# Stick-breaking attention of a decoder step: from cumulative matmuls to a scan along the keys

## The reference

```python
def stick_breaking_weights(z, mask):
    log_beta = jax.nn.log_sigmoid(z)
    log_1m = jnp.where(mask, jax.nn.log_sigmoid(-z), 0.0)
    ax = z.ndim - 1
    tail = lax.cumsum(log_1m, axis=ax, reverse=True) - log_1m
    return jnp.where(mask, jnp.exp(log_beta + tail), 0.0)

z = jnp.einsum('bqhd,bkhd->bhqk', q_blk, k) * scale + bias_f
mask = kpos[None, :] < qpos[:, None]
a = stick_breaking_weights(z, mask)
out = jnp.einsum('bhqk,bkhd->bqhd', a, v)
```

## Time and profile before

| | before |
|---|---|
| median of 3 runs | 3159.7 us (3157.42 to 3159.77) |
| the profiled execution | 3158.64 us |
| its span | 3156.9 us |
| busy in the span | PE 2901.3, DVE 1443.7, ACT 756.3, POOL 1062.1 us |
| mean granted TensorE clock | 0.955 |
| attention's share of the span | about 15% |

### The profile page before, as it was taken

How to read it: one execution, slowest core, us unless ns; L and a number is a source line. 1 busy time by engine, 2 the same in 40 slices (tenths; PEclk the granted TensorE clock), 3 DMA queues, 4 the chain that set the end, 5 groups by cost and what they waited for, 6 DMA issues and landing times.

```text
span 3156.9 us, 44614 instructions
## 1 busy us (share of the span) xinstructions
PE 2901.3 (92%) x16032; PEld 2619.6 (83%) x16032; DVE 1443.7 (46%) x2610; ACT 756.3 (24%) x1575; POOL 1062.1 (34%) x932
## 2 busy tenths in 40 slices
PE   5999769999999999899888888888999999999997
PEld 3777449999999999899885555556989999999997
DVE  5699964422332222641438888860033222222226
ACT  4111061200000000231227777750012000000002
POOL 2478923223333223223214444431032232332320
PEclk9999889999999999999999999985699999999999
DMA  3000001111111111144252222212311111111111
GB/s 118 28 28 21 15 27 47 41 47 41 54 44 43 47 41 54 40 142 129 70 159 61 57 70 67 63 60 94 107 47 47 41 47 48 47 45 43 42 53 56
DMA packets 87684, 183.97 MB, mean 58 GB/s; under 512 B 28995, under 2 KB 43715, under 8 KB 87268
## 3 DMA queue, kind: packets, MB, share of 16 engines
q1 hardware_dynamic: 64260, 145.00, 14.4%
q10 hardware_dynamic: 23264, 36.61, 3.8%
HBM read 150.59 MB, written 30.99 MB: 58 GB/s over the span
## 4 chain that ended last, share of the span: by engine, by line
PE 71%; DVE 14%; issue 8%; ACT 5%; POOL 1%; ACTq 1%; DVEq 1%; DMA 0%; POOLq 0%; SPq 0%
PE bank L1228 48%; PE bank L1332 14%; DVE cv L979 3%; DVE s_sb L1136 3%; PE bank L1483 2%; PE bank L1455 2%; PE bank L1273 1%; DVE sh_sb L1148 1%; DVE xg L924 1%; DVE xl L928 1%; PE bank L1434 1%; DVE ssq L914 1%; ACT sh_sb L843 1%; DVE rstd L1127 1%; POOL s_sb L540 1%
## 5 line engine op out<-in xcount | busy, mean ns | idle before, releaser
L1228 PE MATMUL bank<-xh,wh 128*128 128x352 f32 x3456 | 1131.5, 327 | 32.5 <-DVE xl L928 22.9
L1228 PE MATMUL bank<-xl,wh 128*128 128x352 f32 x3456 | 1117.3, 323 | 0.0
L1228 PE MATMUL bank<-xh,wl 128*128 128x352 f32 x3456 | 1117.1, 323 | 0.0
L497 POOL CAST wh<-w_raw 128x1024 fp32r<-128x1024 f32 x188 | 301.5, 1604 | 1635.3 <-PE bank L1228 1374.7
L1228 PEld LDWEIGHTS bank<-xh,wh 128*128 128x128 f32 x3456 | 654.9, 189 | 45.2 <-DVE xl L928 18.4
L1228 PEld LDWEIGHTS bank<-xl,wh 128*128 128x128 f32 x3456 | 657.4, 190 | 1.8 <-issue 1.7
L1228 PEld LDWEIGHTS bank<-xh,wl 128*128 128x128 f32 x3456 | 656.3, 190 | 0.0
L499 POOL TENSOR_TENSOR wl<-w_raw,wh 128x1024 fp32r<-128x1024 f32 x188 | 456.4, 2428 | 15.1
L1046 DVE TENSOR_TENSOR bank<-bank,sg 128x352 f32<-128x352 f32 x132 | 70.3, 533 | 793.3 <-ACT sg L730 793.3
L1332 PE MATMUL bank<-hh,wh 128*128 128x352 f32 x1056 | 344.0, 326 | 16.4 <-DVE x L1057 13.8
L730 ACT ACTIVATE sg<-bank 128x352 f32<-128x352 f32 x132 | 61.4, 465 | 1200.8 <-PE bank L1228 1200.7
(11 more groups left out here) (136 smaller groups left out, 3056.6 us busy)
## 6 DMA issues: line engine op xcount, KB each, us to landing
w_raw<-wstream SPq DMA_DIRECT2D x188, 512.0 KB, 3.4
k_sb<-k_split SPq DMA_DIRECT2D x16, 512.0 KB, 3.4
qh_sb<-q_split SPq DMA_DIRECT2D x64, 128.0 KB, 2.7
ql_sb<-q_split SPq DMA_DIRECT2D x64, 128.0 KB, 2.8
kp<-cache_kt SPq DMA_DIRECT2D x16, 512.0 KB, 3.5
vp<-cache_v SPq DMA_DIRECT2D x16, 512.0 KB, 3.5
x<-x_t ACTq DMA_DIRECT2D x3, 1408.0 KB, 11.9
k_t<-stage ACTq DMA_DIRECT2D x8, 528.0 KB, 2.8
```

The source lines that it names most:

```text
L497: pool.tensor_copy(wh[:, s], w_raw[:, s % RAW]).then_inc(w_hi, 1)
L1228: mm = pe.matmul(out, a[:, slot, w], b[:, k, tgs(tg)], start=(k == 0 and i == 0), stop=(k == KC - 1 and i == 2))
```

## The change

It turns the scores round: 128 queries lie on the partitions and keys run along the free axis. A head's 36 causal blocks of 128 by 128 are packed into nine chunks of 512 columns (`HEAD_CHUNKS`; a tuple is query block, lowest key block, number of blocks), three of which hold two query blocks; a pair is 18 chunks and the whole is 144. For a chunk:

- PE (`att_z`): the scores by two matmuls a segment, and for a segment that holds the diagonal a third of 128 columns that adds -1e30 where the mask is false. Four score banks instead of six.
- ACT (`att_sigmoids`): sigmoid(z) to SBUF and sigmoid(-z) in place in PSUM.
- DVE (`att_rest`): a scan from the last key down, state = state * sigmoid(-z) + 0, with the state of the segment behind as its start; then (`att_weights`) one multiplication of two SBUF tiles, in place.
- PE (`att_turn`): four transposes of 128 by 128 into one of two banks; ACT (`att_evict`) copies them to SBUF; PE (`att_av`) multiplies with the values in four full-precision matmuls of 128 columns. Both heads of a pair add into the same output banks, whose accumulation is begun by one matmul a pair and bank (chunks 0 and 2); the zero columns between the heads' values make that right.
- The output is rounded and subtracted once a pair and bank, in 128 partitions (before: 64 partitions, once a head and half).

POOL makes the mask's source once and has no other attention work. The clip, exponentials and logarithm, the high and low parts, the cumulative matmuls and the carry go. A head's queries now have a buffer for each of the two heads, the biases are loaded once, and SP, ACT and DVE run straight code. The diff, with the removed functions (printed above) and the bookkeeping left out:

```diff
-EXP_CLIP = 2.0 ** 60
+MASKED = -1e30
 DEC_SPLIT = 6
-NZ = 6
-LEAD = 6
+NZ = 4
+LEAD = 5
+AT_TILES = 3
...
+HEAD_CHUNKS = (
+    ((3, 0, 4),), ((0, 0, 1), (2, 0, 3)), ((5, 2, 4),), ((1, 0, 2), (5, 0, 2)), ((4, 1, 4),), ((6, 3, 4),),
+    ((4, 0, 1), (6, 0, 3)), ((7, 4, 4),), ((7, 0, 4),))
+NCHUNK = len(HEAD_CHUNKS)
+NATT = H * NCHUNK
+PAIR = 2 * NCHUNK
+REST_TILE = {3: 0, 5: 1, 1: 2, 4: 0, 6: 1, 7: 2}
+SMALL_REST = {0: 0, 2: P + 1}
+REST_FREE = {0: -2, 1: -7, 2: -2, 3: 0, 4: 1, 5: 4, 7: 4}
+OUT_CHUNK = {NCHUNK + 3: 0, PAIR - 1: 1}
+class Segment:
+    def __init__(self, qb, low, n, off):
+        self.qb, self.low, self.n = qb, low, n
+        self.off = off
+        self.cols = slice(off, off + n * P)
+        self.first, self.last = low + n == qb + 1, low == 0
+def chunk(g):
+    off, out = 0, []
+    for qb, low, n in HEAD_CHUNKS[g % NCHUNK]:
+        out.append(Segment(qb, low, n, off))
+        off += n * P
+    assert off == QT
+    return out
+def place(g):
+    return g // PAIR, g // NCHUNK % 2, g // NCHUNK
...
-        s_sb = sb("s_sb", [P, 3, QT], F32, r)
-        sh_sb = sb("sh_sb", [P, 3, QT], F32R, r)
-        sl_sb = sb("sl_sb", [P, 3, QT], F32R, r)
-        a_sb = sb("a_sb", [P, 3, QT], F32, r)
-        sb("gap", [P, 2 * (T - SEQ)], F32, r)
+        s_sb = sb("s_sb", [P, NZ, QT], F32, r)
+        at_sb = sb("at_sb", [P, AT_TILES, QT], F32, r)
+        q1_sb = [sb("q1h_sb", [P, SEQ], F32R, r), sb("q1l_sb", [P, SEQ], F32R, r)]
+        mask_r = sb("mask_r", [P, P], F32R, r)
...
+    rest_tiles = [ssq[:], xg[:].rearrange("p a t -> p (a t)"), rstd[:]]
+    small_rest = sq[:].rearrange("p a t -> p (a t)")
+    mask_src = small_rest[:, 2 * TG - P:2 * TG]
+    def rest(seg, first, n):
+        if seg.qb in SMALL_REST:
+            tile, base = small_rest, SMALL_REST[seg.qb]
+        else:
+            tile, base = rest_tiles[REST_TILE[seg.qb]], SEQ - (seg.qb + 1) * P
+        return tile[:, base + first:base + first + n]
...
-    Z = banks[0:NZ]
+    Z, TB = banks[0:NZ], banks[NZ:6]
...
+        def load_head(it, e):
+            h, used = 2 * it + e, PAIR * (it - 1) + NCHUNK * (e + 1)
+            wait_count(sp, Att.z, used)
+            sp.dma_start(k_sb[:, e].bitcast(F32), k_scr[h].rearrange("s d t -> (s d) t")).then_inc(Att.k_in[e], 16)
+            for part in range(2):
+                for half in range(2):
+                    sp.dma_start(q_sb[e][part][DH * half:DH * half + DH, :].bitcast(F32), q_scr[h, part])\
+                      .then_inc(Att.q_in[e], 16)
+            wait_count(sp, Att.av, used)
+            sp.dma_start(v_sb[:, :, 2 * DH * e:2 * DH * e + DH],
+                         v_nat[0:SEQ, h * DH:h * DH + DH].rearrange("(b p) d -> p b d", p=P))\
+              .then_inc(Att.v_in[e], 16)
...
+        pool.wait_ge(n_kv.ready, NTG * KC)
+        pool.memset(mask_src, MASKED).then_inc(Att.mask_src, 1)
+        pool.wait_ge(Att.mask_src, 1)
+        pool.affine_select(out=mask_src, in_=mask_src, compare_op=ALU.is_ge, fill=0.0, base=0,
+                           pattern=[[1, P]], channel_multiplier=-1).then_inc(Att.mask_src, 1)
...
+        def att_sigmoids(g):
+            it, e, h = place(g)
+            act.wait_ge(Att.z, g + 1)
+            wait_count(act, Att.turn, g + 1 - NZ)
+            act.activation(s_sb[:, g % NZ], Z[g % NZ][:], ACT.Sigmoid, bias=b_sb[:, h:h + 1]).then_inc(Att.sig, 1)
+            act.activation(Z[g % NZ][:], Z[g % NZ][:], ACT.Sigmoid, bias=nb_sb[:, h:h + 1], scale=-1.0)\
+               .then_inc(Att.keep, 1)
+        def att_evict(g):
+            act.wait_ge(Att.turn, g + 1)
+            wait_count(act, Att.av, g + 1 - AT_TILES)
+            act.activation(at_sb[:, g % AT_TILES], TB[g % 2][:], ACT.Copy).then_inc(Att.at, 1)
+        def att_out(g):
+            it, qt = g // PAIR, OUT_CHUNK[g % PAIR]
+            act.wait_ge(Att.av, g + 1)
+            act.activation(xh[:, it, qt * QT:(qt + 1) * QT], DN[qt][:], ACT.Copy).then_inc(Att.o_hi, 1)
+        act.wait_ge(Att.const, 2)
+        for slot in range(-LEAD, NATT):
+            if 0 <= slot + 1 < NATT:
+                att_evict(slot + 1)
+            if slot + LEAD < NATT:
+                att_sigmoids(slot + LEAD)
+            if slot >= 0 and slot % PAIR in OUT_CHUNK:
+                att_out(slot)
...
+        def att_rest(g):
+            head = place(g)[2]
+            v.wait_ge(Att.keep, g + 1)
+            if g % NCHUNK in REST_FREE:
+                wait_count(v, Att.a, NCHUNK * head + REST_FREE[g % NCHUNK])
+            for seg in chunk(g):
+                if not seg.first:
+                    v.wait_ge(Att.rest, g)
+                initial = 1.0 if seg.first else rest(seg, (seg.low + seg.n) * P, 1)
+                ins = v.tensor_tensor_scan(rest(seg, seg.low * P, seg.n * P)[:, ::-1], Z[g % NZ][:, seg.cols][:, ::-1],
+                                           zero[:].to_broadcast([P, seg.n * P]), initial, ALU.mult, ALU.add)
+            ins.then_inc(Att.rest, 1)
+        def att_weights(g):
+            v.wait_ge(Att.sig, g + 1)
+            v.wait_ge(Att.rest, g + 1)
+            for seg in chunk(g):
+                tile = s_sb[:, g % NZ, seg.cols]
+                ins = v.tensor_tensor(tile, rest(seg, seg.low * P + 1, seg.n * P), tile, ALU.mult)
+            ins.then_inc(Att.a, 1)
+        def att_out(g):
+            it, qt = g // PAIR, OUT_CHUNK[g % PAIR]
+            cols = slice(qt * QT, (qt + 1) * QT)
+            v.wait_ge(Att.o_hi, 2 * it + qt + 1)
+            v.tensor_tensor(xl[:, it, cols], DN[qt][:], xh[:, it, cols].bitcast(F32), ALU.subtract)\
+             .then_inc(Att.o_lo, 1)
         for n in range(2):
             v.wait_ge(q_stored[n], 4 * 16 * (KC // 2))
+        v.wait_ge(Att.mask_src, 2)
+        v.tensor_copy(mask_r[:], mask_src)
+        v.memset(zero[:], 0.0)
+        for tile in rest_tiles:
+            v.memset(tile[:, SEQ:SEQ + 1], 1.0)
+        for qb, base in SMALL_REST.items():
+            v.memset(small_rest[:, base + (qb + 1) * P:base + (qb + 1) * P + 1], 1.0)
+        v.wait_ge(Att.b_in, 16)
+        v.tensor_scalar(nb_sb[:], b_sb[:], -1.0, None, ALU.mult).then_inc(Att.const, 2)
+        v.wait_ge(Att.const, 2)
+        for slot in range(-LEAD, NATT):
+            if 0 <= slot + LEAD - 1 < NATT:
+                att_rest(slot + LEAD - 1)
+            if 0 <= slot + LEAD - 2 < NATT:
+                att_weights(slot + LEAD - 2)
+            if slot >= 0 and slot % PAIR in OUT_CHUNK:
+                att_out(slot)
...
+        def att_z(g):
+            it, e, h = place(g)
+            if g % NCHUNK == 0:
                 pe.wait_ge(Att.k_in[e], it * 16 + 16)
+                pe.wait_ge(Att.q_in[e], it * 64 + 64)
+            wait_count(pe, Att.rest, g + 1 - NZ)
+            for seg in chunk(g):
+                out, keys = Z[g % NZ][:, seg.cols], k_sb[:, e, seg.low * P:(seg.low + seg.n) * P]
+                queries = slice(seg.qb * P, (seg.qb + 1) * P)
+                pe.matmul(out, q_sb[e][0][:, queries], keys, start=True, stop=False)
+                mm = pe.matmul(out, q_sb[e][1][:, queries], keys, start=False, stop=True)
+                if seg.first:
+                    mm = pe.matmul(Z[g % NZ][:, seg.cols.stop - P:seg.cols.stop], ident_r[:], mask_r[:], start=False,
+                                   stop=True, skip_group_check=True)
+            mm.then_inc(Att.z, 1)
+        def att_turn(g):
             pe.wait_ge(Att.a, g + 1)
+            wait_count(pe, Att.at, g - 1)
+            for b in range(QT // P):
+                cols = slice(b * P, (b + 1) * P)
+                mm = pe.transpose(TB[g % 2][:, cols], s_sb[:, g % NZ, cols], ident[:])
+            mm.then_inc(Att.turn, 1)
+        def att_av(g):
+            it, e, h = place(g)
+            if g % NCHUNK == 0:
+                pe.wait_ge(Att.v_in[e], it * 16 + 16)
+            if g % PAIR == 0:
+                wait_count(pe, Att.o_lo, 2 * it - 1)
+            elif g % PAIR == 2:
+                wait_count(pe, Att.o_lo, 2 * it)
+            pe.wait_ge(Att.at, g + 1)
+            for seg in chunk(g):
+                out = DN[seg.qb // 4][:, seg.qb % 4 * P:(seg.qb % 4 + 1) * P]
+                for b in range(seg.n):
+                    mm = pe.matmul(out, v_sb[:, seg.low + b, DH * e:DH * e + P],
+                                   at_sb[:, g % AT_TILES, seg.off + b * P:seg.off + (b + 1) * P],
+                                   start=(g % PAIR in (0, 2) and b == 0),
+                                   stop=(e == 1 and seg.last and b == seg.n - 1), skip_group_check=True)
+            mm.then_inc(Att.av, 1)
         pe.wait_ge(consts, 8)
         pe.wait_ge(l_q.out, l_q.base + 6 + NTG * KC)
         pe.wait_ge(Att.v_zero, 1)
+        pe.wait_ge(Att.const, 2)
+        for slot in range(-LEAD, NATT):
+            if 0 <= slot + 1 < NATT:
+                att_turn(slot + 1)
+            if slot + LEAD < NATT:
+                att_z(slot + LEAD)
+            if slot >= 0:
+                att_av(slot)
```

(67 more changed lines are left out.)

210 lines of the change are left out of this document (13 added, 197 removed).

## The result

| | before | after |
|---|---|---|
| median | 3158.95 us (3157.42 to 3159.77, 4 runs) | 2984.86 us (2983.74 to 2987.83, 4 runs) |
| span of the profiled execution | 3156.9 us | 2983.7 us |
| attention, first to last VectorE instruction | 458.1 us | 286.3 us |

What follows compares the result with a forecast made beforehand. VectorE at 1.95 us a chunk was taken as the bound, 2.05 with hand-offs. 4.1 + 295.2 + 4.0 + 4.4 = 307.7 against 458.1 us gave 3009 us; own range 2990 to 3040, 8-in-10 range 2980 to 3080.

Steps and rivals of the forecast that it cites:

- to the first scan: Start of attention: constants 1.3, scores and mask at the low clock 1.2, sigmoids 1.3, hops 0.3, together 4.1 us.
- 144 chunks and the low clock: Middle of attention: 2.05 us a chunk, 295.2 us, plus some 4 us lost while the granted clock is low early on.
- after the last scan: End of attention: product, transposes, copy, values, output copy, subtraction and hops, together 4.4 us.
- PE's 1.91 a chunk: Attention on PE: scores, masks, transposes and values sum to 17.2 us a head, or 1.91 a chunk.
- the copy hides under scores and values: PE's slot: about 1.4 us of scores and previous values lies between transposes and the matmuls needing their 0.6 us copy.
- ScalarE's 1.67: Attention on ScalarE, per chunk: two sigmoids 1.14, one weights copy 0.48 and one output copy a head, 1.67 us.
- The scan at 1.20: VectorE's scan of 512 columns: taken as 1.20 us, between bounds of 0.66 and 1.32.
- The rival of the cheap scan: VectorE's scan costs 0.66 us, so PE decides at 1.91 + 0.05 a chunk: 2996 us; chance 20%.
- The dear scan: VectorE's scan costs 1.98 us, by a third pass or slow reversed operand; chunk 2.76, total 3111 us; chance 12%.
- here I allow 0.10: Attention: hand-off loss of 0.10 us a chunk on top of VectorE's 1.95, against 0.32 a step before.
- The rival of a clock that stays low: PE's short matmuls with many weight loads are granted clock 0.50, 3.8 us a chunk: 3257 us, slower; chance 6%.
- The port gain: VectorE's product takes 0.61 us, not 0.99, with GpSimd idle in attention; the rival without it: 3064 us, chance 4%.

Runs made afterwards that it cites:

- the run where it is the bound: The changed kernel without mask matmuls, with every second transpose left out from the third chunk on and half of each scan: 2952.49 us.
- the copy in the open: The changed kernel with PE's value matmuls of a chunk directly behind its transposes, without the next scores between: 3241.99 us.

## Why the prediction was right, and where it was 24 us high

**The 21 us inside attention.** 286.3 us against 307.7. By the prediction's own terms, with the first scan at 1657.23 and the last from 1931.62 to 1932.89:

| term | predicted | measured | difference |
|---|---|---|---|
| to the first scan | 4.1 | 4.84 (1652.39 to 1657.23) | +0.7 |
| 144 chunks and the low clock | 295.2 + 4.0 | 275.7 (1657.23 to 1932.89) | -23.5 |
| after the last scan | 4.4 | 5.8 (1932.89 to 1938.71) | +1.4 |

The stretch also began 1.3 us earlier, at 1652.39 and not at 1653.66; what follows attention kept its length, as predicted (1045.2 us to the end of the span before, 1045.0 after). The rest of the 24 lies between the profiled executions and the medians.

**PE's 1.91 a chunk: right.** 1.918 measured with PE full. The prices (0.23, 0.11 a pass, the load hidden in the stream) held as a sum, and so did the two sub-claims that the copy hides under scores and values and that the loads hide.

**ScalarE's 1.67: right.** 1.69 in the run where it is the bound.

**The scan at 1.20: right, a little high.** Its duration is 1.22 us, but its price in a stream is the distance to the next start, 1803.22 to 1804.35 in the timeline above: 1.13. The whole of VectorE came to 1.87 where the prediction had 1.95; that shows in the run without masks. The Trainium skill, page "DVE: opcode table, instruction layouts, handler registers and perf-mode slots", section "Datapath and trigger behaviour", has the built-in scan at half throughput; the traces agree, 2.08 ns a column against 1.04 for the product. The rival of the cheap scan had the same pace on PE and priced it right (1.91), but for a reason that the rows refute; that its 2996 lies nearer to the result than 3009 is luck. The dear scan falls with the row of 1.22 us, and its slow reversed operand with the forward scan. That rival's sum was also too low by its own terms: 2.59 and the forecast's extras of 0.24 are 2.83 a chunk and not 2.76, about 3121 and not 3111.

**The step that failed: "here I allow 0.10".** The prediction took the longest engine, VectorE at 1.95, and added 0.10 for hand-offs, scaled down from the 0.32 a step that VectorE lost before. Both parts were high. VectorE's 1.95 was 0.08 us too much, so that PE, at 1.918, was the longest; and the hand-off allowance should have been nothing: (2.05-1.918) x 144 = 19 us of the 24. So the prediction named the wrong engine as the bound. That this cost so little is luck: its sums for the two engines, 1.95 and 1.91, happened to lie 0.04 apart. With PE at its bare sum and no loss to the low clock its own terms give 3009 - 20 - 4 = 2985, which is the result; it called that case the edge of its range and put it at 2980. What the old kernel lost I put down to loops (PE for the exponential, ScalarE for the clip, VectorE for the rounding), in which one step's latency comes round to a later step; that is argued from its waits, and no run took such a loop out of it. In the new one the scores are five chunks ahead, and PE needs no result within the slot in which it asked for it. An allowance carried over from a kernel with other loops had no basis here; the run with the copy in the open shows the opposite case, where a loop closes, and there it is 1.8 us a chunk, not 0.1.

**The low clock: 4 us predicted, about 1.4 measured.** The clock was low, 0.67 over 1654 to 1664: 0.50 up to 1658, 0.95 and 0.90 in the next two stretches of 2 us, in which PE stood idle for 2.01 and then 0.61 us before transposes, and 0.50 again in 1662 to 1664. Until the first transposes, at 1660.26, PE had only the scores of four chunks to do, from 1653.22 to 1658.25; ScalarE, behind its table load, began on them at 1655.89 and found all four ready. The price comes after that:

```profile
1662.05 1.11 PE L1358 MATMUL bank<-ident,s_sb 128*128 128x128 f32 x4 [0.61 <-DVE s_sb L1089]
...
1665.39 0.60 PE L1358 MATMUL bank<-ident,s_sb 128*128 128x128 f32 x4
```

From one chunk's transposes to the next it is 3.34 us here, where the next distance is 1.90: 1.4 us. From the first transposes to the last, at 1934.91 below, it is 274.65/143 = 1.921 us a chunk, only 0.003 over the pace of the middle, because the first slot, which has no values to do, and the last ones, which have no scores, gave most of that back.

**After the last scan, 4.4: a chunk short.** The timeline of the end:

```profile
1931.62 1.27 DVE L1078 TENSOR_TENSOR_SCAN rstd<-bank,rstd,zero 128x512 f32<-128x512 f32 x1
...
1932.81 1.27 DVE L1089 TENSOR_TENSOR s_sb<-rstd,s_sb 128x512 f32<-128x512 f32 x2
...
1934.91 0.60 PE L1358 MATMUL bank<-ident,s_sb 128*128 128x128 f32 x4
1935.35 2.01 PE L1374 MATMUL bank<-at_sb,v_sb 128*128 128x128 f32 x16
...
1938.02 0.69 DVE L1096 TENSOR_TENSOR xl<-bank,xh 128x512 fp32r<-128x512 f32 x1 [3.95 <-ACT xh L798]
```

Two products and the values of two chunks (x16, 2.01 us) follow the last scan, since the scan runs ahead of the product and the product ahead of PE. I had counted one of each.

**The rival of a clock that stays low** is refuted: 1.00 through 1700 to 1900 with 1624 matmuls of 128 to 512 columns, each with its own weights; decode still has its 0.50 with PE full.

**The port gain**, as the prediction calls it, is shown from both sides, with the product at 671 ns, and at 1176 when GpSimd is put back beside it.

**Not foreseen:** the sigmoid's table load of 1.28 us on the path to the first scan. It is the 0.7 us by which the start was off, and half a microsecond more that the other terms of the start gave back.
